# Gathers and scatters of a mixture of experts as half rows over 128 partitions, with the slots spread

## The reference

```python
gp, gi = lax.top_k(group_probs, 1)                 # the best of 4 groups
ev, ei = lax.top_k(elog, EXPERT_TOPK)              # the 2 best of its 8 experts
ew = jax.nn.softmax(ev, axis=-1) * gp
...
a = jnp.einsum('nd,edf->nef', xt, w_gate[sl])      # 1024 -> 256
b = jnp.einsum('nd,edf->nef', xt, w_up[sl])        # 1024 -> 256
hh = jax.nn.silu(a) * b * comb[:, sl, None]
y = y + jnp.einsum('nef,efd->nd', hh, w_down[sl])  # 256 -> 1024
```

## Time and profile before

| what | us |
|---|---|
| median of 3 runs (917.64 to 921.09) | 918.93 |
| profiled execution | 918.71 |
| its span, first to last instruction | 917.0 |
| PE busy / DVE busy / ACT busy / POOL busy | 826.7 / 322.8 / 223.2 / 188.3 |

### The profile page before, as it was taken

The page is one execution under the profiler, slowest core; times in us unless marked ns, Lnnn a source line. Parts: engine busy times, 40 slices in busy tenths (PEclk is TensorE's granted clock), DMA queues, the critical chain, the costliest instruction groups (busy, mean ns, idle before and its releaser), DMA issues.

```text
span 917.0 us, 11639 instructions
## 1 busy us (share of the span) xinstructions
PE 826.7 (90%) x4517; PEld 512.2 (56%) x4517; DVE 322.8 (35%) x879; ACT 223.2 (24%) x457; POOL 188.3 (21%) x257
## 2 busy tenths in 40 slices
PE   5989999999899989999999999994999999787860
PEld 3464344688566755675766774554555555455430
DVE  4222656998544531123222363437100000000005
ACT  3021332112333323333333511112122222111110
POOL 2223440000332222100000011001244434323230
PEclk9999999999999999999999999995999999999995
DMA  8424020421200200303040497118999999999957
GB/s 281 147 93 121 4 93 1 143 92 51 93 0 1 93 1 0 99 1 138 1 93 1 153 413 299 47 65 320 377 387 384 385 377 377 381 397 397 380 206 292
DMA packets 53672, 164.60 MB, mean 180 GB/s; under 512 B 14192, under 2 KB 16464, under 8 KB 44880
## 3 DMA queue, kind: packets, MB, share of 16 engines
q1 hardware_dynamic: 46432, 149.79, 44.4%
q0 software_dynamic: 7184, 14.06, 4.5%
HBM read 153.58 MB, written 18.08 MB: 187 GB/s over the span
## 4 chain that ended last, share of the span: by engine, by line
PE 75%; DMA 11%; DVE 4%; POOL 3%; ACT 3%; issue 2%; SPq 2%; POOLq 0%; DVEq 0%; ACTq 0%
PE quad L781 25%; PE pair L1112 9%; DMA arena<-in_w_up 6%; PE pair L1330 5%; PE pair L975 5%; PE quad L1330 4%; PE quad L849 3%; DMA hreg<-in_w_up 3%; PE quad L1341 3%; PE pair L771 2%; PE quad L1069 2%; PE pair L1341 2%; POOL arena L1759 2%; PE quad L1323 1%; PE pair L896 1%
## 5 line engine op out<-in xcount | busy, mean ns | idle before, releaser
L781 PE MATMUL quad<-ring_w,xnT 128*128 128x512 f32 (+1 forms) x192 | 79.3, 553 | 0.0
L1812 POOL DMA_INDIRECT y_d<-ring_w,idx_y x64 | 57.7, 902 | 72.4 <-ACT ring_w L1638 60.3
L975 PE MATMUL pair<-xnT,ring_w 128*128 128x272 f32 x256 | 70.3, 410 | 0.9 <-POOLq L1765 0.9
L1112 PE MATMUL pair<-xnT,ring_w 128*128 128x272 f32 x256 | 65.8, 403 | 0.0
L781 PE MATMUL quad<-xnT,ring_w 128*128 128x280 f32 (+1 forms) x256 | 60.6, 396 | 0.0
L1330 PE MATMUL quad<-arena,ring_w 128*64 128x256 f32 x384 | 48.1, 407 | 9.1 <-DMA arena<-in_w_up 8.4
L975 PEld LDWEIGHTS pair<-xnT,ring_w 128*128 128x128 f32 x256 | 46.4, 192 | 16.8 <-issue 7.9
L1112 PEld LDWEIGHTS pair<-xnT,ring_w 128*128 128x128 f32 x256 | 46.5, 189 | 15.3 <-issue 6.9
L781 PEld LDWEIGHTS quad<-xnT,ring_w 128*128 128x128 f32 x256 | 48.2, 190 | 11.3 <-issue 0.8
L1330 PE MATMUL pair<-arena,ring_w 128*64 128x256 f32 x384 | 45.8, 392 | 9.5 <-DMA arena<-in_w_up 9.1
L2051 DVE CUSTOM_DVE_ANT_0 arena<-quad,arena 128x528 f32<-128x528 f32 (+4 forms) x34 | 17.7, 521 | 103.9 <-PE quad L1167 60.9
(11 more groups left out here) (268 smaller groups left out, 1255.6 us busy)
## 6 DMA issues: line engine op xcount, KB each, us to landing
arena<-in_w_gate SPq DMA_DIRECT2D x24, 1024.0 KB
arena<-in_w_up SPq DMA_DIRECT2D x24, 1024.0 KB
arena<-in_w_down SPq DMA_DIRECT2D x40, 512.0 KB
ring_w<-in_w_in SPq DMA_DIRECT2D x8, 2048.0 KB, 8.6
ring_w<-in_w_down SPq DMA_DIRECT2D x20, 512.0 KB
xnT<-in_w_gate SPq DMA_DIRECT2D x4, 1024.0 KB
xnT<-in_w_up SPq DMA_DIRECT2D x4, 1024.0 KB
hreg<-in_w_gate SPq DMA_DIRECT2D x4, 1024.0 KB
```

The costliest lines, as they stand in the source:

```text
L781: last = nc.tensor.matmul(o, l, r, start=i == 0, stop=i == len(mms) - 1)
L975: last = nc.tensor.matmul(bank[6 + job % 2][:, 0:hi - lo], chunk8(6 + cb // 4)[:, k, c0:c0 + P], xT[:, k, lo:hi], start=k == 0, stop=k == ...
L1112: last = nc.tensor.matmul(bank[6 + job % 2][:, 0:hi - lo], w[:, k, c0:c0 + P], rhs[:, k, lo:hi], start=k == 0, stop=k == kt - 1)
L1812: pool.indirect_dma_start(y_d, bass.IndirectOffsetOnAxis(ap=rows, axis=0), Yb[64 * c:64 * c + 64, q, :], None, bounds_check=4 * NTOK - 1, ...
```

## The change

The rows of x are stored with their columns in another order (first the columns whose number modulo 8 is 0 to 3, then the others), so that a row is two half rows, and a gather takes both: partition p of 128 gets half p // 64. Which slot a partition holds is set by `spread`: with m = p % 64 it is slot m % 8 * 8 + m // 8, so that slots s and s + 1 lie 8 partitions apart. Both gathers in flight lie side by side in `Xg` (two times 512 columns). The turned x takes four products of 128 x 128. y is scattered by one DMA of 128 half rows. The index lists have 128 partitions, `slot_at` has 128 columns and lives in `cst`, `idx_y` is one list whose second half has 2 added, and rows of y lie as half 0 of both choices, then half 1 of both; the final sum reads them so. `second_norm` is two instructions of half the columns, and `x2_turned` waits for each.

```diff
...
         for choice in range(2):
-            c[:TOK[t], K_RID + choice * NT + n] = 4 * (TOFF[t] + i[:TOK[t]]) + 2 * choice - NO_ROW
+            c[:TOK[t], K_RID + choice * NT + n] = 4 * (TOFF[t] + i[:TOK[t]]) + choice - NO_ROW
     c[:, K_IOTA:K_IOTA + CAP] = np.arange(CAP)
+    m = np.arange(P) % CAP
+    c[:, K_SPREAD:K_SPREAD + P] = m % 8 * 8 + m // 8
+    c[:, K_YROW] = NO_ROW + 2 * (i // CAP)
     c[:, K_THR:K_THR + 8] = CAP * (1 + np.arange(8))
...
         wslot = [ring_w[:, s * 4096:(s + 1) * 4096] for s in range(2)]
-        Xg = ring_w[:, 4 * D:5 * D]
+        Xg = ring_w[:, 4 * D:5 * D].rearrange("p (i c) -> p i c", i=2)
         Yb = ring_w[:, 6 * D:7 * D].rearrange("p (i d) -> p i d", i=2)
-        xgT = ring_w[:, 7 * D:8 * D].rearrange("p (i k s) -> p i k s", i=2, k=KT)
+        xgT = ring_w[:, 7 * D:8 * D].rearrange("p (i j h s) -> p i j h s", i=2, j=4, h=2)
         hid, sil, hidT = (cst[:, K_COS + 256 * i:K_COS + 256 * (i + 1)].rearrange("p (i c) -> p i c", i=2) for i in range(3))
...
         picks = gate7[:, 64:192].rearrange("p (c i e) -> p c i e", c=2, i=2)
-        slot_at = gate7[:, 192:448].rearrange("p (i c s) -> p i c s", i=2, c=2)
+        slot_at = cst[:, K_COS:K_COS + 4 * P].rearrange("p (i c s) -> p i c s", i=2, c=2)
...
         slot_i = sb("slot_i", 2 * NT, I32)
-        idx_x = sb("idx_x", NBLK, I32, CAP)
-        idx_y = [sb(f"idx_y{c}", NBLK, I32, CAP) for c in range(2)]
-        idx_now = [sb(f"idx_now{c}", 1, I32, CAP) for c in range(3)]
+        idx_x = sb("idx_x", NBLK, I32)
+        idx_y = sb("idx_y", NBLK, I32)
+        idx_now = [sb(f"idx_now{c}", 1, I32) for c in range(2)]
         over_i = sb("over_i", MAX_OVER + 1, I32, 1)
...
         xn2_d = nc.dram_tensor("xn2_d", [NTOK, D], F32).ap()
+        xn2_half = xn2_d.rearrange("r (h c) -> (r h) c", h=2)
         h_d = nc.dram_tensor("h_d", [NTOK, D], F32).ap()
...
-                    sp.wait_ge(x2_ready, NT)
+                    sp.wait_ge(x2_ready, 2 * NT)
                     sp.wait_ge(h_out, 16 * NT)
...
                 r = TOK[ORDER[i]]
-                pe.wait_ge(x2_ready, i + 1)
-                xk = x2row[0:r, i % 2, :].rearrange("p (c k) -> p k c", k=KT)
-                for q in range(2):
-                    tr_job([(xk[:, 4 * q + j, :], ident[0:r, 0:r]) for j in range(4)], r)
+                xk = x2row[0:r, i % 2, :].rearrange("p (h c j) -> p h j c", h=2, j=4)
+                for h in range(2):
+                    pe.wait_ge(x2_ready, 2 * i + h + 1)
+                    tr_job([(xk[:, h, j, :], ident[0:r, 0:r]) for j in range(4)], r)
...
                 for c in range(2):
-                    last = nc.tensor.matmul(bank[7][0:CAP, 0:NE], slot_at[0:r, j, c, :], rid_at[0:r, j, c, :],
+                    last = nc.tensor.matmul(bank[7][:, 0:NE], slot_at[0:r, j, c, :], rid_at[0:r, j, c, :],
                                             start=i == 0 and c == 0, stop=i == NT - 1 and c == 1, skip_group_check=True)
...
                 for n in range(2 * NT):
-                    last = nc.tensor.matmul(bank[7][0:CAP, NE:NBLK], at_slot[:, n, :], at_block[:, n, :],
-                                            start=n == 0, stop=n == 2 * NT - 1, skip_group_check=True)
+                    for h in range(2):
+                        last = nc.tensor.matmul(bank[7][CAP * h:CAP * (h + 1), NE:NBLK], at_slot[:, n, :],
+                                                at_block[:, n, :], start=n == 0, stop=n == 2 * NT - 1,
+                                                skip_group_check=True)
                 last.then_inc(over_idx_ready, 1)
...
             def x_to_width(q, done):
-                qp = slice(CAP * q, CAP * (q + 1))
-                x = Xg[qp, :].rearrange("p (c k) -> p k c", k=KT)
-                for k in range(KT):
-                    last = nc.tensor.transpose(bank[4 * q][:, k * CAP:(k + 1) * CAP], x[:, k, :], ident[qp, qp])
+                x = Xg[:, q, :].rearrange("p (c j) -> p j c", j=4)
+                for j in range(4):
+                    last = nc.tensor.transpose(bank[4 * q][:, P * j:P * (j + 1)], x[:, j, :], ident)
                 last.then_inc(done, 1)
...
                             bank[4 * q + 1][64 * f:64 * f + 64, 0:256].rearrange("p (g c) -> p g c", g=2),
-                            xgT[:, q, k, :], wv[:, :, k, P * f:P * (f + 1)], start=k == 0, stop=k == KT - 1)
+                            xgT[:, q, k % 4, k // 4, :], wv[:, :, k, P * f:P * (f + 1)], start=k == 0, stop=k == KT - 1)
                 last.then_inc(done, 1)
...
             def copy_x(q, done):
-                nc.scalar.activation(xgT[:, q], bank[4 * q].rearrange("p (k s) -> p k s", k=KT), ACT.Copy)\
+                nc.scalar.activation(xgT[:, q].rearrange("p j h s -> p (j h s)"), bank[4 * q], ACT.Copy)\
                     .then_inc(done, 1)
...
-                pool.wait_ge(x2_ready, i + 1)
+                pool.wait_ge(x2_ready, 2 * i + 2)
                 pool.dma_start(xn2_d[TOFF[t]:TOFF[t] + TOK[t], :], x2row[0:TOK[t], i % 2, :]).then_inc(x2_stored[t], 16)
...
             def gather(q, rows, done):
-                pool.indirect_dma_start(Xg[CAP * q:CAP * (q + 1), :], None, xn2_d, bass.IndirectOffsetOnAxis(ap=rows, axis=0),
-                                        bounds_check=NTOK - 1, oob_is_err=False).then_inc(done, 16)
-            def scatter(q, c, rows):
-                pool.indirect_dma_start(y_d, bass.IndirectOffsetOnAxis(ap=rows, axis=0), Yb[64 * c:64 * c + 64, q, :], None,
+                pool.indirect_dma_start(Xg[:, q, :], None, xn2_half, bass.IndirectOffsetOnAxis(ap=rows, axis=0),
+                                        bounds_check=2 * NTOK - 1, oob_is_err=False).then_inc(done, 16)
+            def scatter(q, rows):
+                pool.indirect_dma_start(y_d, bass.IndirectOffsetOnAxis(ap=rows, axis=0), Yb[:, q, :], None,
                                         bounds_check=4 * NTOK - 1, oob_is_err=False).then_inc(y_out[q], 16)
...
                 pool.wait_ge(y_copied, n + 1)
-                for c in range(2):
-                    scatter(n % 2, c, idx_y[c][:, n:n + 1])
+                scatter(n % 2, idx_y[:, n:n + 1])
...
                 gather(n, idx_x[:, n:n + 1], gath[n])
-            pool.wait_ge(idx_in, 2)
             for n in range(NE):
...
                 dve.wait_ge(rstd2_ready, i + 1)
-                nc.vector.scalar_tensor_tensor(x2row[0:r, i % 2, :], X[0:r, t, :], rstd[0:r, t:t + 1], g2b[0:r, :],
-                                               ALU.mult, ALU.mult).then_inc(x2_ready, 1)
+                x2 = x2row[0:r, i % 2, :].rearrange("p (h c j) -> p h c j", h=2, j=4)
+                for h in range(2):
+                    nc.vector.scalar_tensor_tensor(x2[:, h], X[0:r, t, :].rearrange("p (c h j) -> p h c j", h=2, j=4)[:, h],
+                                                   rstd[0:r, t:t + 1],
+                                                   g2b[0:r, :].rearrange("p (c h j) -> p h c j", h=2, j=4)[:, h],
+                                                   ALU.mult, ALU.mult).then_inc(x2_ready, 1)
...
                 red(slot_here[0:r, :, 0:n], picks[0:r, :, 0:n], ALU.add)
-                here = slot_here[0:r, :, 0:n].rearrange("p c (i o) -> p c i o", o=1).broadcast_to([r, 2, n, CAP])
+                here = slot_here[0:r, :, 0:n].rearrange("p c (i o) -> p c i o", o=1).broadcast_to([r, 2, n, P])
                 tt(slot_at[0:r, j0:j0 + n].rearrange("p i c s -> p c i s"),
-                   iota[0:r].rearrange("p (c i s) -> p c i s", c=1, i=1).broadcast_to([r, 2, n, CAP]), here, ALU.is_equal)
+                   spread[0:r].rearrange("p (c i s) -> p c i s", c=1, i=1).broadcast_to([r, 2, n, P]), here, ALU.is_equal)
                 nc.vector.sem_inc(slots_ready, n)
...
-                got = bank[7][0:CAP, lo:hi]
-                ts(idx_y[0][:, lo:hi], got, float(NO_ROW), None, ALU.add)
-                nc.vector.tensor_scalar(idx_x[:, lo:hi], idx_y[0][:, lo:hi], 2, None, ALU.logical_shift_right).then_inc(o, 1)
-                nc.vector.tensor_scalar(idx_y[1][:, lo:hi], idx_y[0][:, lo:hi], 1.0, None, ALU.add).then_inc(o, 1)
+                ts(idx_y[:, lo:hi], bank[7][:, lo:hi], y_row0, None, ALU.add)
+                nc.vector.tensor_scalar(idx_x[:, lo:hi], idx_y[:, lo:hi], 1, None, ALU.logical_shift_right).then_inc(o, 1)
...
                 r = TOK[t]
-                for c in range(2):
-                    n = 2 * t + c
-                    if c == 0:
-                        dve.wait_ge(h_in[t], 16)
-                        dve.wait_ge(comb_in[t], 16)
-                    link(nc.vector.scalar_tensor_tensor(X[0:r, t, :], arena[0:r, n * D:(n + 1) * D],
-                                                        ew[c][0:r, ORDER.index(t):ORDER.index(t) + 1], X[0:r, t, :], ALU.mult, ALU.add))
+                dve.wait_ge(h_in[t], 16)
+                dve.wait_ge(comb_in[t], 16)
```

(36 more changed lines are left out.)

6 lines of the change are left out of this document (2 added, 4 removed).

## The result

The changed kernel takes 908.79 us (median of 4 runs, 908.31 to 908.96), the kernel before, measured beside it, 918.28: a ratio of 0.989 (0.987 to 0.992). Its profiled execution has a span of 907.0 us, 10 less than before. That the range came so near is luck, since its lower end stood for rival 1, which the runs refute (e1, e2).

What follows compares the result with a forecast made beforehand. The prediction took the weight stream, landing last on the slowest DMA engine, as the bound. Its terms, 6.0 − 1.0 + 0.9 − 0.7 − 0.1 = +5.1 us, gave 924.0 us for the median, range 909 to 928.

Steps and rivals of the forecast that it cites:

- rival 1: Gathers and scatters: eight neighbouring partitions per engine, slowest engine −7.3 to −8.5 us, 910.5 to 911.7 us; chance 0.30.
- What bounds the kernel: Experts' stage: the weight stream never pauses; the end is the last `in_w_up` landing on the slowest engine, plus 36 us.
- case (a): Gathers and scatters: an engine takes four neighbouring partitions and four further up; slowest engine +38 rows, 6.0 us; chance 0.38.
- pairs: Gathers and scatters: engines take partitions in groups of two; slowest engine +48 rows, +7.6 us, 926.6 us; chance 0.12.
- The price of unevenness, +6.0 us: Slowest DMA engine at the last weights: more rows in the new slot order, +6.0 us, taken between fours and pairs.
- 0.158 us: Price of one 4 KB row on a DMA engine, read from the weight queue at 25.9 GB/s.
- The bytes stay: Gathers and scatters: the same bytes move as before; no size was given.
- The relief, −1.0 us: End of the weight stream: loaded engines speed up once light ones finish, at most 2.3 us back, taken as −1.0.
- The lead of the light engines, 33 us: End of the weight stream: light engines finish 209 rows, 33 us, ahead, not stopping earlier since enough loads are queued.
- GpSimd: Issue of gathers and scatters: 1.4 us each for 128 rows; −0.7 us after the last y.
- the term of +0.9: Two first gathers between the indices and the load of slot 6: 2 × 0.45 = +0.9 us (0 to +1.8).
- Ahead of the indices: Before the indices: x2 in halves −0.6 us, `slot_at` +0.3, four index products +0.2; together −0.1 us.

Runs made afterwards that it cites:

- e1: The changed kernel with its slots in natural order in each half of the partitions; 900.91 us, 0.980 of before.
- e2: The changed kernel with slots dealt out so that, by the map of fours, every engine holds one slot of each eight; 897.71 us, 0.977 of before.
- e7: e2 with the four products that turn x done twice for each expert; 898.1 us.
- e3: The kernel before with only its slot order changed, spread evenly over the engines' pairs of partitions; 911.15 us, 0.990 of before.
- e10: e2 with the gather of x cut in two of 64 partitions; 913.18 us, 0.994 of before.
- e5: e1 with the gather of x cut in two of 64 partitions; 917.53 us, 0.998 of before.
- e9: e1 with x gathered by two transfers over all 128 partitions, of 1 KB quarter rows each; 905.79 us.
- e4: e1 with the scatter of an expert cut in two of 64 partitions; 902.58 us.
- e12: e1 with one more unread gather for each of experts 5 to 31, into partitions 32 to 95; 919.2 us.
- e11: e1 with one more unread gather for each of experts 5 to 31, into partitions 0 to 63; 930.0 us.

## Why the prediction was wrong, point by point

**What bounds the kernel: right.** In every version the end followed the last `in_w_up`, and 24 us more of TensorE changed nothing (e7).

**The map, case (a): right.** Eight engines loaded, eight light: the half-full windows from 872 to 880 us show that much, and the share of 0.49 in the last scatter rules out pairs. The Trainium skill (DMA: Bandwidth & Descriptors, "The descriptor swizzle") gives this map for a plain transfer; here the trace shows it for an indirect scatter of 128 partitions, and for a gather too. The changed kernel's first gather (34 rows) runs from 638.3 to 639.8 us, ahead of the full stream. By its packet records four engines carry one half row and then three packets of two empty slots each, as fours have it; by pairs two engines would carry two half rows each. Rival 1, which rested on eight neighbours per engine, fell; four neighbours and four more are eight per engine too.

**The price of unevenness, +6.0 us: the sign right, the size between two readings.** It can now be read against even orders: the kernel before loses 8.0 us to its order (e3), the changed kernel 11.1 (e2), so the order costs 3.1 us more than before; against the natural order of the same transfers it is 7.9 (e1), where 47 rows at 0.158 us give 7.4. The single steps scatter: 34 rows gave 8.0 us (e3), 45 rows 3.2 us (e2 against e1), 36.5 rows 4.4 (e10 against e5). The most loaded engine's rows give sign and order of size, not the microsecond. What they miss was not tried.

**"The bytes stay", and with them the duration of a packet: this step failed.** The sum took the stream's 387 GB/s over unchanged and had no term for it. The step from 384 to 413 GB/s over the 241 us from 640 to 881 us is 241 × (1 − 384/413) = 16.9 us. The narrow gather measured 16.6 us (e5 against e1) and 15.5 us (e10 against e2), with a second gather to issue in each; against e9, which has two as well, it is 11.7. The cause is the span of the gather. It wrote 64 partitions within one half, 0 to 63 or 64 to 127, and while such a gather is carried out, the packets beside it take longer. The trace of before showed it, in windows that I had not made. Here the kernel before from 692 to 696 us; GpSimd issued a gather at 689.04 us and two scatters at 691.53 and 692.73:

```profile
692.00:693.00 1.00, 1.00 (x14) 0.64 (x12) 0.00 (x0) 0.00 (x0) 0.70 (x2) 1.00 1.03 422
693.00:694.00 1.00, 1.00 (x11) 0.47 (x8) 0.00 (x0) 0.00 (x0) 0.64 (x1) 1.00 1.09 344
694.00:695.00 1.00, 1.00 (x10) 0.93 (x12) 0.29 (x1) 0.28 (x1) 0.00 (x0) 1.00 1.01 299
695.00:696.00 1.00, 1.00 (x6) 0.41 (x8) 0.00 (x0) 0.60 (x1) 0.20 (x1) 1.00 1.01 410
```

The share stays at 1.0 and more, and the rate drops to 344 and 299 GB/s, for about two of the 6.8 us of an expert. Every 8 KB packet that started between 693.5 and 694.5 us took 416 to 573 ns, by the packet records, where 313 is the median. (Against 413 GB/s the two microseconds lose 0.18 MB, 0.44 us; with 30 gathers in the stream that is 13 us, an estimate from one landing.) The dip belongs to the gather and not to the scatters issued around it: its landing signals come from 695.06 to 696.08 us, those of the scatters from 697.17 us on, and e4 and e5 say the same. The gather before it, into the other half, has its dip at 687 us, 225 GB/s.

The Trainium skill (SBUF — State Buffer, "Door 1: The DMA port swizzle") says that partitions 0 to 63 reach only eight of the 16 ports by which DMA gets into SBUF, no more than 0 to 31, and that the other eight belong to 64 to 127. For the span of a transfer the runs agree at three places: 32 partitions cost as 64 do (383 and 384 GB/s), 128 cost nothing (413), and 32 to 95 cost nothing either (413). For the place of the rows they do not: by the same rule 32 to 63 have no other ports than 0 to 31, and rows there cost nothing in e12 while rows in 0 to 31 cost rate in e11. So the ports of the rows alone do not explain it. Whether it is which engine writes which port is open. The Trainium skill's section on the descriptor swizzle, cited above, has each engine keep to one port in a 128-partition transfer, which would explain why wide gathers and weights do not meet; that step no run here shows. The Trainium skill's rule of Door 1 (SBUF — State Buffer) bears on "the bytes stay", and the prediction did not weigh it.

**The relief, −1.0 us: wrong, and its evidence was the missed clue.** I read 24.2 GB/s per engine with all at work and 25.9 with two as crowding. It was not: with all 16 at work and no narrow gather an engine moves 413/16 = 25.8 GB/s, with eight 25.8. The 7% between the two rows was the narrow gather's tax, present in the one stretch and absent in the other.

**The lead of the light engines, 33 us: wrong.** They stood still for about 9 us at the end, and earlier the rate was down to 390 GB/s from 740 us on, where e1 keeps 413. So they pause on the way as well. Between 740 and 870 us 414 against 386 GB/s is 8.8 us, and half of the 8 us at the end 4.0: 12.8 against the 11.1 measured. The step that failed is "loads for the next six or seven are queued". A load lands about 25 us after its issue, 26.06 in the changed kernel's chain: three experts' time, and less than 33 us. SP, in the changed kernel:

```profile
656.11 0.82 SPq L698 DMA_DIRECT2D arena<-in_w_down  x2
...
776.90 2.91 SPq L694 DMA_DIRECT2D arena<-in_w_up  x1
779.86 3.21 SPq L698 DMA_DIRECT2D arena<-in_w_down  x2
...
785.02 7.08 SPq L698 DMA_DIRECT2D arena<-in_w_down  x2
```

Two issues that took 0.82 us take 3 to 7 us later, one behind the other, while from 700 to 870 us SP waits only 19 us for PE to free a slot. So it is mostly the issuing and not the slots that holds the loads back. Why an issue then takes so long was not tried.

**GpSimd: the size off, the direction right.** A gather or scatter over 128 partitions takes 1.02 us, not 1.4. At the tail 2.10 us became 1.02, −1.1 instead of −0.7; ahead of the stream the term of +0.9 shrinks to +0.1.

**Ahead of the indices: −0.1 predicted, +0.9 measured, by another row.** The x2 halves gave about −0.3 (instead of −0.6), `slot_at` took 0.69 as expected, and the eight index products took 1.91 us for 1.06: I had priced four of them, at +0.2. The load of slot 6 went out at 641.47 us, 0.9 late, close to the +0.8 that the two wrong terms happened to give together (+0.9 and −0.1).

**The sum as measured.** The new transfers in natural order −18.2 us (919.13 to 900.91), the new slot order +7.9: −10.3, against 918.28 − 908.79 = 9.5 in the direct comparison. Of the −18.2, 11.7 to 16.6 are the span of the gather and 1.7 the one scatter (e4); what is left is not split further.

## What to carry to other kernels

Let an indirect gather that runs beside a full stream span partitions on both sides of 64 in one transfer; it is worth more here than everything else in this change. Put the busy slots where the DMA map spreads them: for 128 partitions an engine has four neighbours and the four 32 higher, so neighbouring slots belong in different fours, not 8 partitions apart. When two stretches of one trace show an engine at different rates, find out which is the disturbed one before pricing either, and look at the rate at full DMA share in windows of 1 us.

## What the hardware showed that I had not expected

- A gather whose span of 32 or 64 partitions lies in one half slows the packets beside it: 344 and 299 GB/s in two microseconds of one such gather, at a full share, 383 to 384 against 413 GB/s on average. The same gather over partitions 32 to 95 does not, even when all its rows land below 64 (390 and 414 GB/s in e11 and e12).
- A scatter from 64 partitions of one half does not (413 GB/s in e4).
- Descriptors for 128 rows cost GpSimd 1.02 us against 0.97 for a gather of 64.
- Eight DMA engines at work move half of what 16 move (206 and 414 GB/s).
- Under a full stream two load issues of SP take 3 to 7 us in place of 0.82, and a load lands 24 to 26 us after its issue in the chains shown.
